# Sums of weight blocks made in DRAM, and two blocks split by one instruction, in a one-core hybrid encoder layer

## What is computed

```
h  = RMSNorm(x) * (1 + scale1(c)) + shift1(c)
P  = h @ w_in                       # mixer A, q, k, v, z, gates
yA = W_aout( Bg * dwconv3( Cg * hA ) )
yB = W_bout( GatedRMSNorm( GatedDeltaRule(conv4(q,k,v)), z ) )   # 8 heads
x  = x + gate1(c) * W_o( sigmoid(gA) * yA + sigmoid(gB) * yB )
h  = RMSNorm(x) * (1 + scale2(c)) + shift2(c)
x  = x + gate2(c) * W2( relu(h W1)^2 )      # W1: 1024 x 4096, W2: 4096 x 1024
y  = RMSNorm(x) * (1 + scale_f(c)) + shift_f(c)
```

## Time and profile before

| | |
|---|---|
| median of 3 runs | 1277.05 us (1272.19 to 1278.63) |
| profiled execution | 1275.4 us, span 1273.7 us |
| PE busy | 1214.7 us, 95% of the span |
| VectorE, ScalarE, GpSimd busy | 756.9, 480.5, 203.6 us |
| bytes by DMA | 156.58 MB, mean 123 GB/s |

### The profile page before, as it was taken

One profiled execution on the slowest core, in us unless ns is written; L12 is line 12 of the kernel. 1 busy time (PEld: TensorE's weight loads), 2 busy tenths in 40 slices (PEclk: granted clock), 3 DMA queues, 4 the chain that ended last, 5 costly groups with the idle time before them and its releaser, 6 DMA issues.

```text
span 1273.7 us, 26942 instructions
## 1 busy us (share of the span) xinstructions
PE 1214.7 (95%) x11304; PEld 1154.5 (91%) x11304; DVE 756.9 (59%) x1158; ACT 480.5 (38%) x894; POOL 203.6 (16%) x347
## 2 busy tenths in 40 slices
PE   6999999999999999999999999999799889989986
PEld 3899999999999999999999999799789889988986
DVE  5676656454554545537769964667546555654655
ACT  4574433232222322233343333544324433433454
POOL 4011112103021030111100010014300320230241
PEclk8999999999999999999999999999999999989998
DMA  9632233213122121328745647146853873694583
GB/s 327 226 83 71 80 85 92 61 43 85 51 83 60 48 75 51 93 69 249 229 133 165 238 167 248 51 132 126 153 120 100 145 138 99 123 163 112 109 141 94
DMA packets 224075, 156.58 MB, mean 123 GB/s; under 512 B 6090, under 2 KB 211372, under 8 KB 222680
## 3 DMA queue, kind: packets, MB, share of 16 engines
q1 hardware_dynamic: 182932, 109.56, 29.7%
q0 software_dynamic: 40768, 45.26, 17.3%
q10 hardware_dynamic: 260, 0.10, 0.0%
HBM read 149.00 MB, written 5.90 MB: 122 GB/s over the span
## 4 chain that ended last, share of the span: by engine, by line
PE 81%; DMA 11%; DVE 3%; ACT 2%; issue 2%; SPq 1%; DVEq 0%; ACTq 0%; POOLq 0%
PE gp L790 49%; PE gp L1196 15%; DMA w_raw<-in_w_ff 10%; PE gp L1234 3%; PE dp L1020 2%; DVE w_lo L2230 1%; PE dp L1030 1%; DMA ada_w<-in_ada_w 1%; ACT w_hi L1653 1%; PE gp L816 1%; PE dp L1087 1%; PE dp L1053 1%; PE dp L1080 1%; PE dp L1072 1%; PE dp L1032 1%
## 5 line engine op out<-in xcount | busy, mean ns | idle before, releaser
L790 PE MATMUL gp<-a_hi,w_hi 128*128 128x288 f32 x1408 | 312.1, 303 | 0.3 <-DVE w_lo L1781 0.3
L790 PE MATMUL gp<-a_hi,w_lo 128*128 128x288 f32 x1408 | 301.5, 296 | 0.0
L790 PE MATMUL gp<-a_lo,w_hi 128*128 128x288 f32 x1408 | 301.3, 296 | 0.0
L790 PEld LDWEIGHTS gp<-a_hi,w_hi 128*128 128x128 f32 x1408 | 224.8, 189 | 11.6 <-issue 6.1
L790 PEld LDWEIGHTS gp<-a_hi,w_lo 128*128 128x128 f32 x1408 | 226.7, 189 | 0.0
L790 PEld LDWEIGHTS gp<-a_lo,w_hi 128*128 128x128 f32 x1408 | 226.5, 189 | 0.0
L1781 DVE TENSOR_TENSOR w_lo<-w_raw,w_hi 128x1024 fp32r<-128x1024 f32 x98 | 120.2, 1227 | 101.2 <-ACT w_hi L1324 100.3
L1234 PE MATMUL gp<-f_hi,w_hi 128*128 128x288 f32 x448 | 140.1, 313 | 37.2 <-ACT keep L1687 29.5
L2230 DVE TENSOR_TENSOR w_lo<-w_raw,w_hi 128x512 fp32r<-128x512 f32 (+1 forms) x126 | 101.9, 816 | 82.4 <-ACT w_hi L1653 81.3
L1234 PE MATMUL gp<-f_lo,w_hi 128*128 128x288 f32 x448 | 137.0, 306 | 0.0
L1234 PE MATMUL gp<-f_hi,w_lo 128*128 128x288 f32 x448 | 136.6, 305 | 0.0
(11 more groups left out here) (345 smaller groups left out, 1760.7 us busy)
## 6 DMA issues: line engine op xcount, KB each, us to landing
w_raw<-in_w_in SPq DMA_DIRECT2D x72, 512.0 KB, 3.8
w_raw<-in_w_ff SPq DMA_DIRECT2D x48, 512.0 KB, 4.1
ada_half<-in_ada_w POOLq DMA_DIRECT2D x32, 512.0 KB, 4.6
w_raw<-in_w_ff POOLq DMA_DIRECT2D x48, 256.0 KB, 5.3
ada_w<-in_ada_w SPq DMA_DIRECT2D x16, 512.0 KB, 9.8
w_raw<-in_w_ff SPq DMA_DIRECT2D x32, 256.0 KB, 3.5
w_raw<-in_w_a_out SPq DMA_DIRECT2D x8, 512.0 KB, 4.3
w_raw<-in_w_b_out SPq DMA_DIRECT2D x8, 512.0 KB, 4.0
```

Source lines behind the costliest of these rows:

```text
L790: last = T_.matmul(gp[:, 2 * b + h, 0:HALF], wp[:, b, k, :], ap[:, k, h * HALF:(h + 1) * HALF], start=(k == 0 and wp is w_hi and ap is hi) ...
```

## The change

The sums of W2's blocks no longer come into being in SBUF during the down stages. A DRAM tensor `w_sums` of 4 kinds x 4 quarters holds them all; POOL makes them there with 64 DMAs of 512 KB, 32 copies and 32 accumulating ones (`weight_sums`): one after each of the 24 projection tiles, nine in each of the four groups of the delta rule, four at its end. They go in 18 batches, and a batch waits for the DMAs of the batch two before (`sums_made`). SP loads each block, sum or not, into the next half buffer of `w_raw`, eight halves in a ring, as soon as the block eight places earlier is split. In the down stages one ACT instruction and one DVE instruction of 1024 columns split two neighbouring blocks; they wait until both blocks before them in those halves are done. The parts of f are released in three steps a unit (`parts_before`), and the sums of f of the up pair ahead of a down stage are made inside that stage (`first_sum`, `other_sums`, `sums_hi`, `sums_lo`); those of the last unit in four steps.

```diff
+    stages = (("copy1", "copy3"), ("add1", "add3"), ("copy2",), ("add2",), ("copy4",), ("add4",))
+    plan = [(j + 2 * n, kind, j) for n, kinds in enumerate(stages) for j in range(8) for kind in kinds]
...
-    w_s3 = sb("w_s3", [P, 4, P], at=r_ds + 25984)
...
+    w_sums = nc.dram_tensor("w_sums", [4, 4, P, 4, 4, P], F32, kind="Internal").ap()
...
+    def pair_of(t, k):
+
+        n = RAW if t is w_raw else 2
+        return t[:, ITEMS[k][3] // 2 % n, :, :]
...
+        for k in range(2, len(ITEMS)):
+            p, name, width, at = ITEMS[k]
+            if at < 2 * RAW:
+                sp.wait_ge(S["w_lo_done"], N_FF - RAW + (at + width) // 2)
             else:
+                last = max(m for m in range(len(ITEMS)) if ITEMS[m][3] < at + width - 2 * RAW)
+                sp.wait_ge(S["w_lo_done"], N_FF + last + 1)
+            if name[0] == "s":
+                for batch in (2 * PAIRS[p][1] + 10, 2 * PAIRS[p][1] + 11):
+                    sp.wait_ge(sums_made[batch % 2], 16 * sums_before(batch + 1, batch % 2))
+            sp.dma_start(raw_block(k), w_block(p, name)).then_inc(landed(k)[0], 16)
...
+        def weight_sums(first, last):
+
+            for n in range(first, last):
+                batch, kind, j = SUMS[n]
+                if n == 0 or SUMS[n - 1][0] != batch:
+                    if batch > 1:
+                        pool.wait_ge(sums_made[batch % 2], 16 * sums_before(batch, batch % 2))
...
             pads(2 * g + 1)
+            weight_sums(NQKV + 9 * g, NQKV + 9 * g + 6)
             tails_of(2 * g + 1)
+            weight_sums(NQKV + 9 * g + 6, NQKV + 9 * g + 9)
...
             for u in units:
                 if i == 0:
-                    pe.wait_ge(S["f_split"], 4 * q + u + 1)
+                    pe.wait_ge(S["f_split"], parts_before(4 * q + u, blk))
...
             p, name, width, at = ITEMS[k]
+            if width == 1 and at % 2 == 0:
+                return
             if at + width - 4 > 0:
                 act.wait_ge(S["slot_done"], at + width - 4)
...
+            if width == 1:
+                act.wait_ge(*landed(k - 1))
+                act.wait_ge(*landed(k))
+                AC(pair_of(w_hi, k), pair_of(w_raw, k), ACT.Copy).then_inc(S["w_hi_done"], 2)
+                return
...
+            if q < 3 and i == 0 and name == "w22":
+                sums_hi(p - 1)
...
+            if width == 1:
+                TT(pair_of(w_lo, k), pair_of(w_raw, k), pair_of(w_hi, k).bitcast(F32), ALU.subtract).then_inc(S["w_lo_done"], 2)
+                return
```

More of the change, by code:

```diff
@@ L101, with sum_plan, sums_before @@
 END = {(p, name): at + width for p, name, width, at in ITEMS}
+def sum_plan():
+    stages = (("copy1", "copy3"), ("add1", "add3"), ("copy2",), ("add2",), ("copy4",), ("add4",))
+    plan = [(j + 2 * n, kind, j) for n, kinds in enumerate(stages) for j in range(8) for kind in kinds]
+    return sorted(plan, key=lambda step: step[0])
+SUMS = sum_plan()
+def sums_before(batch, parity):
+    return sum(b < batch and b % 2 == parity for b, _, _ in SUMS)
 def issued(k):
@@ L319, in build @@
     ADA_IN = 32
-    first_full, second_full, sum_full, s3_full = ada_full[0:2], ada_full[2:4], ada_full[4:6], ada_full[6]
-    sum_added, s3_added = [nc.alloc_semaphore(f"sum_added{i}") for i in range(2)], nc.alloc_semaphore("s3_added")
+    half_full = ada_full
+    sums_made = [nc.alloc_semaphore(f"sums_made{i}") for i in range(2)]
     GROUPS = [(2 * g, 2) for g in range(KT // 2)] + [(KT, 1)]
@@ L367, in split_items, with w_block, raw_block, landed @@
         return N_FF + NTH[p, name] + 1
-    def w_block(p, name, tile=0):
+    def w_block(p, name):
         kind, q, i = PAIRS[p]
         if kind == "up":
-            c = q * D + (2 * i + tile) * P
+            c = q * D + (2 * i + "ab".index(name)) * P
             return w_ff1.rearrange("(k p) n -> p k n", p=P)[:, :, c:c + P]
+        if name[0] == "s":
+            return w_sums[int(name[1]) - 1, q, :, i]
         c = (2 * i + (name in ("w21", "w22"))) * P
         v = w_ff2.rearrange("(k p) n -> p k n", p=P)[:, q * KT:(q + 1) * KT, c:c + P]
-        if name == "w1":
-            return v
         return v.rearrange("p (m e) c -> p e m c", e=2)[:, 0 if name in ("w11", "w21") else 1]
[L381 to L394, removed]
+    def raw_block(k):
+        _, _, width, at = ITEMS[k]
+        v = w_raw.rearrange("p s (h k) c -> p (s h) k c", h=2)
+        return w_raw[:, at // 2 % RAW, :, :] if width == 2 else v[:, at % (2 * RAW)]
+    def pair_of(t, k):
+        n = RAW if t is w_raw else 2
+        return t[:, ITEMS[k][3] // 2 % n, :, :]
+    def landed(k):
+        h = ITEMS[k][3] % (2 * RAW)
+        return half_full[h], ADA_IN + 16 * sum(at % (2 * RAW) == h for _, _, _, at in ITEMS[2:k + 1])
+    def parts_before(j, blk):
+        return 3 * j + {3: 1, 0: 1, 2: 2, 1: 2, 4: 3, 5: 3, 6: 3}[blk] + (j == 15 and blk > 4)
     def slots(t, k):
@@ L400, in slots @@
         return t[:, at // 2 % 2, :, :] if width == 2 else v[:, at % 4]
[L402 to L408, removed]
     block = nc.Block()
@@ L633, in conv_edges @@
                 conv_edge(i, b)
-        with pool.Fori(0, NQKV // 2) as i:
+                weight_sums(2 * i + b, 2 * i + b + 1)
+        for i in range(NQKV // 2):
             conv_edges(i)
@@ L735, in _ @@
             pool.tensor_tensor(shift[:, e, :], shift[:, e, :], final_b[:, :], ALU.add).then_inc(S["shift_done"], 1)
[L737 to L765, removed]
+        pool.wait_ge(S["mod_done"], 3)
+        pool.wait_ge(S["slot_done"], END[DOWN[-4] - 1, "b"])
+        for e in range(2):
+            for f in range(2):
+                pool.tensor_scalar(diag[:, e, f, :], ident[:, :], scales[:, 2, KT - 2 + f, e:e + 1], None, ALU.mult)\
+                    .then_inc(S["diag_done"], 1)
         pool.wait_ge(S["tail_sb"], 2)
@@ L1718, in _ @@
                 up_hi(p, tile)
+                if tile and p + 1 not in DOWN[:12]:
+                    sums_hi(p)
                 if p == 1 and tile:
@@ L2320, in _ @@
                 up_step(p, "ab".index(name), issued(k))
+                if name == "b" and p + 1 not in DOWN[:12]:
+                    if ups(p) < 15:
+                        first_sum(ups(p))
+                    other_sums(ups(p))
+                    sums_lo(ups(p))
                 if p == 4 and name == "a":
@@ L2325, in _ @@
             down_step(p, name, issued(k))
+            if q < 3 and i == 0 and name == "s4":
+                first_sum(ups(p - 1))
+                other_sums(ups(p - 1))
+            elif q < 3 and i == 1 and name == "w12":
+                sums_lo(ups(p - 2))
             if q == 3 and i and name == "s2":
```

127 lines of the change are left out of this document (68 added, 59 removed).

## The result

The changed kernel takes 1232.68 us, the median of 4 runs (1232.44 to 1232.73 in three of them), against 1274.8 before: a ratio of 0.9667, with a 95% interval of 0.9629 to 0.9704.

The account below looks back on a forecast made before the run. PE was taken to lose some 56 us in down stages because ACT waits for accumulating DMAs sharing a half buffer. 1275.4 - 45.2 (down stages) + 1 (front) + 4 (hand-offs) = 1235.2, so 1235 us; range 1222 to 1258.

Parts of the forecast that it names:

- the walk: Chain followed through the four down stages: 46.0 us for each of the first three, 53.3 for the last, 191.3 together.
- the part that is not matmul: Down stages of the kernel before: 12.6 to 15.7 us in each of the first three, some 56 us in all four.
- The allowance: Hand-offs and queueing left out of the walk, on 56 pairs of blocks: 4 us taken, from 0 to 28 possible.
- The pair split: Down stages, splits of 1024 columns: ready at 2.7 or 3.0 us, PE arrives at 3.15, so they fit.
- Sums of f: Same work in other places: priced by the walk where late for a product, nothing inside up tiles.
- Front: 64 DMAs in projections and delta rule, at most 2.75 us an addition, under POOL's waits: nothing to 7 us, 1 taken.
- The saturation rival: Sums saturate the DMA engines in the delta rule, deciding at 108 ns a packet; slower, above 1282 us; chance 0.08.
- What was to be seen: New profile: no ACT transfer wait in down stages, clock 1.00 there, no POOL DMA after 570 us but late adaLN loads.

Follow-up runs that it names:

- the best version: The change with splits of 512 columns and ACT and PE work reordered at the last down stage's start and the program's end: 1224.74 us.
- the start reordered: The change with splits of 512 columns; in the last down stage, keep5 and keep1 precede f's last high parts, tail rows follow keep2: 1227.31 us.

## Why the prediction was right

**The total.** Forecast 1235, measured 1232.68; the profiled execution fell by 42.7 us where 40.2 were forecast. The down stages fell by 42.9 where the walk and its allowance left 41.2. The rest of the program cost 0.2 us more than before, where 1 was forecast, and that these are close is luck: the cost allowed at the front did not come, but the first up stage behind a down stage took 51.3 us instead of 50.2, which no term foresaw. One reading is off without a consequence: the part that is not matmul was 13.1 to 15.7 us in the first three stages, not 12.6; the 56 in all are right.

**Down stages.** The walk gave 46.0 three times and 53.3; measured 46.7, 46.7, 47.0 and 53.1. Two things differ in the first three: the pace of a stage is 0.1325 us a matmul and not the 0.1314 of the first 36 (336 x 0.0011 = 0.4), and the waits come to 2.2, 2.2 and 2.5 us a stage, not 1.8. The places were mostly as walked: 0.75 us at s3 of the last pair (forecast 0.7), 0.23 and 0.22 at w22 of the second and s1 of the fourth pair (0.2 each), 0.17 where keep1 stands behind `sums_hi` (0.4; in the third stage 0.50). Not in the walk is a gap of 0.27 at a stage's end. In the last stage 1.17 and 1.02 us at s2 and s1 (1.1 each) and 1.22 in the last pair (1.4).

**The allowance.** "I take 4" for what the walk left out: the stages sum to 193.6, 2.3 above the walk's 191.3. It was 2 us too much, and the range from 0 to 28 was far too wide at its upper end.

**The pair split.** The step costed it as fitting "with 0.1 to 0.4 us to spare", and it does fit. What the step left out is the comparison: it walked only the new form, not the same kernel with splits of 512, and so did not see that the pair split costs 6 us. Its list of waits named the reason (subtractions and keeps behind 1.23 and 1.06 us), and with splits of 512 most of them go.

**Sums of f.** "The same work in other places", priced where late. The move's worth, 6.6 us, is part of the walk's numbers but was not set apart.

**Front.** 1 us was taken; the first down stage begins 0.4 us earlier, and without the DMAs not earlier still: nothing beyond the spread of some 1.5 us. The bound of 2.75 us for an addition was twice what POOL takes, 1.30; all of it lay under POOL's waits, so the size does not show.

**The saturation rival** was rightly held to be unlikely, and it was no phantom: forecast to decide at 108 ns a packet where 47 were expected, about 2.3 times the load, it did cost 30 us at twice the load. POOL's masks came late as described, but at another wait: POOL stood at its issues until its own DMAs had landed, not at `sums_made`. The load was right by luck. The delta rule's share rose by 0.36 x 360 = 130 us of all engines where 41 DMAs of 1024 packets at 47 ns gave 123; but the trace has 27,069 packets more there, 660 a DMA, and POOL's queue, with 27,357 packets at 36.5%, spent 77 ns on each. Fewer and dearer packets make the same load; neither factor was right. SP's 512-KB loads paid in the projections, 3.8 to 5.9 us; in the delta rule they went from 3.9 to 4.1, and to 6.4 with the DMAs twice. The Trainium skill ("DMA: Bandwidth & Descriptors", section "Issuing engines are not separate DMA queues") says that transfers of different issuers interleave on the same 16 engines; these rows agree.

**What was to be seen** came: ACT waits for no transfer in a down stage, the clock there is 1.00, and no sum is issued after 570 us.

## What to carry to other kernels

A sum that depends on weights alone can be made in DRAM long before it is needed, as long as the queue that makes it and the DMA engines have idle time there; measure that room by issuing it twice. Merging two short instructions into a long one saved 1.9 us of ACT's busy time a down stage here (21.1 for 23.0), on an engine that isn't the bound, and lengthened the hand-offs behind it, 1.0 to 1.5 us a stage on PE; price it against the unmerged form of the same kernel, not only against the kernel before. Where the bounding engine stands 2 us, count what the clock may take after it, not the wait alone.

## What the runs showed that was not expected

- The end of the program can pay for a short wait twice. In the change PE waits 1.3 us for the last squares, and the granted clock of the stretch behind is 0.57; in the best version it waits for nothing there, and the clock is 1.00. The wait alone doesn't fix the price: after the same 1.3 us the clock of these matmuls was 0.84 with splits of 512 alone and 0.51 with the start reordered. The stretches, of the change and of the best version:

```profile
1219.20:1223.80 4.60, 4.51 (x36) 3.31 (x36) 2.14 (x2) 0.49 (x3) 0.00 (x0) 0.57 0.56 228
```

```profile
1210.50:1215.40 4.90, 4.85 (x82) 4.25 (x80) 3.34 (x5) 2.23 (x8) 0.00 (x0) 1.00 0.11 41
```

- The same up stage of 384 matmuls, without a gap, takes 50.0 us in one place of the kernel before and 51.3 in its other one and in the change, at a granted clock of 1.00 in all of them. The median distance of two starts is the same, 0.131 us; but in the slow ones 93 to 95 of the distances are 0.140, and in the quick one none is, while 160 are 0.128. No run tells why.
